# Moving the last weight tile's low part on VectorE behind the first scaled tile, at four transitions between phases

## The reference, cut to what matters

```
mix = ... @ w_out                       # or  ff = (silu(gate) * val) @ w_down
x = x + rms_norm(mix, gain_post)        # the transition: square, sum over width, root, scale, add
u = rms_norm(x, gain_next)              # input of the next phase
... = u @ w_next
```

## Time and profile before

| what | us |
|---|---|
| median of 3 executions | 1779.47 |
| lowest and highest of them | 1779.31, 1780.46 |
| the profiled execution | 1781.4 |
| its span, first to last instruction | 1779.6 |
| PE busy in it | 1709.4 (96%) |
| DVE busy in it | 1076.9 (61%) |
| ACT busy in it | 852.0 (48%) |

### The profile page before, as it was taken

How to read it: one execution, slowest core, us unless ns; L and a number is a source line. 1 busy time by engine, 2 the same in 40 slices (tenths; PEclk the granted TensorE clock), 3 DMA queues, 4 the chain that set the end, 5 groups by cost and what they waited for, 6 DMA issues and landing times. The chain is left out here.

```text
span 1779.6 us, 23788 instructions
## 1 busy us (share of the span) xinstructions
PE 1709.4 (96%) x8312; PEld 1385.3 (78%) x8312; DVE 1076.9 (61%) x1688; ACT 852.0 (48%) x1450; POOL 432.2 (24%) x332
## 2 busy tenths in 40 slices
PE   7999999999999999899999998999999989999997
PEld 5777887877888888778888887888888866677775
DVE  5536454377566633688788848666653376787343
ACT  5656545354333332456556545333332255355562
POOL 0443454101111100135555520111110013222231
PEclk9999999999999999999999999999999999999999
DMA  5322111222222222311221222222323223221121
GB/s 204 113 71 72 36 36 66 72 77 98 102 95 94 94 94 94 106 60 50 70 72 52 68 83 71 83 94 95 101 89 103 95 71 111 71 72 48 48 71 48
DMA packets 40516, 144.78 MB, mean 81 GB/s; under 512 B 4578, under 2 KB 4834, under 8 KB 39924
## 3 DMA queue, kind: packets, MB, share of 16 engines
q1 hardware_dynamic: 40436, 143.72, 23.8%
HBM read 141.57 MB, written 2.13 MB: 81 GB/s over the span
## 5 line engine op out<-in xcount | busy, mean ns | idle before, releaser
L187 PE MATMUL bank<-u_high,w_high 128*128 128x512 f32 x1580 | 646.6, 409 | 15.3 <-DVE m_on L1938 3.2
L189 PE MATMUL bank<-u_high,w_low 128*128 128x512 f32 x1580 | 619.3, 392 | 0.0
L188 PE MATMUL bank<-u_low,w_high 128*128 128x512 f32 x1580 | 618.8, 392 | 0.0
L187 PEld LDWEIGHTS bank<-u_high,w_high 128*128 128x128 f32 x1580 | 298.9, 189 | 94.3 <-issue 30.1
L189 PEld LDWEIGHTS bank<-u_high,w_low 128*128 128x128 f32 x1580 | 298.3, 189 | 65.2
L151 ACT ACTIVATE w_high<-w_ring 128x1024 fp32r<-128x1024 f32 x233 | 244.0, 1053 | 213.0 <-PE bank L189 168.5
L188 PEld LDWEIGHTS bank<-u_low,w_high 128*128 128x128 f32 x1580 | 299.2, 189 | 58.6 <-issue 3.8
L160 DVE TENSOR_TENSOR w_low<-w_ring,w_high 128x1024 fp32r<-128x1024 f32 x176 | 220.8, 1257 | 179.5 <-ACT w_high L151 179.2
L160 POOL TENSOR_TENSOR w_low<-w_ring,w_high 128x1024 fp32r<-128x1024 f32 x57 | 136.3, 2403 | 474.9 <-ACT w_high L151 474.9
L881 ACT ACTIVATE conv_up<-bank,col_sb 128x512 f32<-128x512 f32 x88 | 68.6, 780 | 270.5 <-DVE bank L936 270.5
L996 POOL TENSOR_TENSOR hidden<-conv_up 128x512 f32 x44 | 58.2, 1324 | 493.9 <-DVE conv_up L947 373.7
(11 more groups left out here) (410 smaller groups left out, 2273.6 us busy)
## 6 DMA issues: line engine op xcount, KB each, us to landing
w_ring<-ffn_up SPq DMA_DIRECT2D x88, 512.0 KB, 3.4
w_ring<-ffn_down SPq DMA_DIRECT2D x44, 512.0 KB, 3.4
w_ring<-c_in SPq DMA_DIRECT2D x32, 512.0 KB, 3.5
w_ring<-g_in SPq DMA_DIRECT2D x16, 512.0 KB, 3.8
w_ring<-m_in SPq DMA_DIRECT2D x12, 512.0 KB, 5.8
w_ring<-fox_in SPq DMA_DIRECT2D x12, 512.0 KB, 4.1
w_ring<-dsa_in SPq DMA_DIRECT2D x12, 512.0 KB, 3.4
w_ring<-ab_out SPq DMA_DIRECT2D x8, 512.0 KB, 4.7
```

The source lines that it names most:

```text
L187: nc.tensor.matmul(out, a[0], b[0], start=start, stop=False)
L188: nc.tensor.matmul(out, a[0], b[1], start=False, stop=False)
L189: return nc.tensor.matmul(out, a[1], b[0], start=False, stop=stop)
```

## The change

In all four transitions DVE makes the low part of tile 2 where it did, and that of tile 3 after both halves of tile 0 have been scaled and added, before scale(1). No instruction is added or removed, and no wait is changed.

```diff
@@ half_out @@
-            for s in range(2, 4):
-                k.split_low(dve, s, KD + s)
+            k.split_low(dve, 2, KD + 2)
             for i, c in enumerate(parts):
                 dve.wait_ge(rooted, i + 1)
                 scale(0, c)
                 add(0, c, i)
+            k.split_low(dve, 3, KD + 3)
             for m in range(1, KD):
                 scale(m)
                 op.low(dve, m - 1)
@@ ffn @@
-            for s in range(2, 4):
-                k.split_low(dve, s, KF + s, other=s == 2)
+            k.split_low(dve, 2, KF + 2, other=True)
             for i, c in enumerate(parts):
                 dve.wait_ge(rooted, i + 1)
                 scale(0, c)
                 add(0, c, i)
+            k.split_low(dve, 3, KF + 3)
             for m in range(1, KD):
                 scale(m)
                 op.low(dve, m - 1)
```

## The result

The ratio of the changed kernel's time to before's is 1.0018, with a 95% interval of 1.0011 to 1.0025: 0.18% slower, as forecast, on the edge of what can be told from no change. The medians of twelve executions each are 1783.20 us (1781.97 to 1785.31) and 1780.34 (1778.94 to 1781.93), 2.9 us apart. The profiled execution of the changed kernel took 1782.95.

A forecast was written before the change was run, and what follows sets the result against it. DVE's queue, as a chain from scale(0) to the gather, was taken to set the pace, not PE. 2 x 1.07 + 2 x 0.56 = +3.26 us on 1779.47 gave 1782.7 us, range 1781.0 to 1784.6.

The forecast's parts named there:

- the 3.26 of the sum: All four transitions: net cost 2 x 1.07 + 2 x 0.56 = +3.26 us.
- The phase's end hangs on the gather: Transition ends: L306 waits for DVE's last gather addition, so a gather shift moves the next phase one for one.
- 1.14 us for the moved low part, not 1.22: Behind add(0), ahead of scale(1): the low part adds 1.14 us per transition, as neighbours overlap by 0.08.
- What its going gives back: 0.07 in half_out, 0.58 in ffn: Ahead of scale(0): without the low part it starts earlier, by 0.07 us in half_out and 0.58 in ffn.
- ab, 1.07: Half_out transition ab: net cost on DVE's chain 1.14 - 0.07 = +1.07 us.
- the second half follows 0.92 after the first: Scaling in ab: the second half starts 0.92 us after the first, at 374.84, so it too gains 0.07.
- One transition's upper bound was 1.14: Each transition: if the earlier scaling gave nothing back, the cost is 1.14 us, in all 4.56.
- PE's earlier opening at nothing: PE's first product: 0.07 or 0.58 us earlier, counted as no gain because PE then waits ahead of L306.
- Rival A: Openings: PE is the path, its first product comes earlier by 0.07 or 0.58 us, time 1778.2; chance 0.05.
- Rival B: Chain steps: DVE's idle time, up to 1.4 us, takes up the shift, time stays at 1779.5; chance 0.05.
- Rival C: Transition ends: PE's clock falls, 1.6 us per fall; 1784.3 for one, 1787.5 for three; chance 0.09.
- Rival D: Ahead of scale(0): the scaling gains nothing, full price 4.56 us, time 1784.0; chance 0.06.

The follow-up runs named there:

- after_again: The changed kernel run once more without an edit: 1782.68 us against 1780.67 for the kernel before, ratio 1.0014.
- both_behind: Changed kernel with tile 2's low part also put behind add(0), in all four transitions: 1787.69 us, ratio 1.0042 to the kernel before.
- ffn_only: The kernel before with the move made in the two ffn transitions alone: 1781.37 us, ratio 1.0006 to the kernel before.
- pe_two_after: Changed kernel with two products more on PE in each opening: root-to-next-phase distances 30.31, 29.78, 29.78 and 29.81 us; no whole time given.
- pieces: Kernel before, with tile 3's low part in both ffn transitions cut up, 384 columns before scale(0), five pieces later: 1779.68 us, ratio 0.9998.
- pool_tile3: Changed kernel with tile 3's low part made by POOL instead of DVE: 1787.02 us, ratio 1.0038 to the kernel before.

## Why the prediction was right

The direction, the place and the mechanism held, and so did the size: ratio 1.0018 measured, 1782.7 / 1779.47 = 1.0018 forecast. That the two agree to the last digit is partly luck. The distances in the profiles grew by 3.67, more than the 3.26 of the sum, and the medians by 2.9 here and 2.0 in after_again, less than it; the two deviations have different causes.

- *The phase's end hangs on the gather.* Shown: L306 to the next phase is 5.05 us before and after, and the gather's shift arrives whole.
- *1.14 us for the moved low part, not 1.22.* Right: 375.36 to 376.50. The second low part of both_behind cost 1.12 to 1.13. By the Trainium skill's rule (VectorE: DVE Perf Modes, "The DRAIN you can't avoid") it would have been 1.22; here the measurement decides. The same section adds, which the prediction passed over, that an operation that is not held (one that need not wait until every earlier one has finished) starts earlier; the rows agree with that.
- *What its going gives back: 0.07 in half_out, 0.58 in ffn.* Right for scale(0) in all four, which starts 0.03 after its root. The distances of c and both ffn came out within 0.02 us.
- *ab, 1.07.* This is the mis-sized term: 1.45. The step that failed is "the second half follows 0.92 after the first", which was carried over from a queue that ran without a break. It was 1.30, and without the wait on x_back 0.87, as its removal showed; what makes that wait dear here and not in both_behind is open. One transition's upper bound was 1.14, and ab passed it; only the sum stayed inside.
- *PE's earlier opening at nothing.* Right for the changed kernel, as ffn_only and pe_two_after show. PE's first product came 0.58, 0.08 and 0.58 us earlier after the root in the first ffn, c and the second ffn, as forecast. In ab it came 0.30 later (376.51 - 373.88 before, 376.04 - 373.11 after) where 0.07 earlier was forecast, since the wait on x_back stands in front of u_high(0) as well. PE's idle time ahead of L306 came to 1.46 in ab and 1.59 in the first ffn, for 1.36 and 1.37 forecast; in ab that is two errors that cancel, a gather 0.38 later than forecast behind an opening 0.37 later.
- *Rival A*, PE as the path, fell for the changed kernel, but it had a point that the prediction missed: in the kernel before, PE had 0.4 us in hand with a short low stretch and none with a long one. Two profiles in three of before had one such opening, 0.4 to 0.5 us longer. There the change costs correspondingly less. That goes the right way to bring the 3.67 of the distances down to the 2.9 and 2.0 of the medians, but how often it happens in executions without a profile was not seen, so it is a likely cause and not a shown one.
- *Rival B* fell with both_behind, though pieces shows that the idle time in the steps is real: it takes work that is put into it, and not a late start.
- *Rival C* did not come about: in none of the thirteen profiles did the clock fall behind the L306 of ab, c or the first ffn, up to 1.65 us of idle time ahead of it. Nor does "2.0 us did it" hold as a rule, since the same wait of 2.0 us brought no fall in eight profiles of thirteen. *Rival D* is out, since scale(0) moved to its root.

## What to carry to other kernels

On an engine whose queue is the path, moving an instruction from in front of a wait to behind it doesn't hide it: it turns the time in which the engine would have worked into idle time, and the chain behind pays the difference. Compare the moved instruction's length with the time by which it kept the engine busy after the wait was met; here it was 1.14 us against 0.07 and 0.58. If the work must go, cut it to the size of the chain's idle slots, or give it to an engine that doesn't share a port with the one relieved. An engine that is 96% busy can still be the one that waits, at the few places that set the end.

## What the runs showed of the hardware

- A GpSimd operation with SBUF inputs stops a scalar_tensor_tensor of VectorE with two SBUF inputs for as long as it runs: 0.48 us became 2.23 and 1.68.
- TensorE's low clock after the idle time ahead of an opening lasted 3.4 us in most profiles and 6.8 in some, or did not come at all, even at one and the same place of one and the same program (three profiles of before: 3.4, 6.8, 6.8 in the second ffn, and 3.4, none, none in c).
- A semaphore wait that was met long before cost VectorE 0.4 us in front of add(0) in four profiles of the changed order and in pool_tile3, and 0.06 in the old order and in both_behind.
